# Eight-core hybrid trunk (pooling mixer and gated linear attention): launch, unit changes, gate input, sums of squares and end rearranged

## The reference

```
h = concat(meta, x)
for i in range(4):
    h = h + (pool_mixer, gla_mixer)[i % 2](rmsnorm(h, norm[i]))
out = rmsnorm(h, final_norm)[:, 16:]

pool_mixer: u, z = split(h @ w_in)                       # 2048 channels each
            t = trailing_mean(u, w) - u                  # w = 2, 4, 8, 16 by group of 512 channels
            y = (t @ w_grp[g]) * scale * silu(z);  return y @ w_out
gla_mixer:  q, k, v, z, glr = split(h @ w_in)            # 4 heads, dk 256, dv 512, glr of rank 16
            log_a = log_sigmoid(glr @ w_gate2 + b) / 16
            by chunk: cum = cumsum(log_a); qe = q*exp(cum); ke = k*exp(-cum)
                      o = mask(qe ke^T) v + qe S;  S = exp(g_tot)*S + (k*exp(g_tot-cum))^T v
            o = o * rsqrt(mean(o^2) + eps) * head_norm * silu(z);  return o @ w_out
```

## Time and profile before

| what | us |
|---|---|
| time, median of 3 runs | 2346.13 |
| the three runs | 2346.13, 2355.87, 2049.5 |
| profiled execution, its own time | 2046.73 |
| its span, slowest core (2039.7 to 2045.2 over the cores) | 2045.2 |
| TensorE's mean granted clock, over the cores | 0.994 to 0.997 |
| busy on the slowest core: PE, DVE, ACT, POOL | 1949.3, 1540.1, 1147.1, 258.6 |

### The profile page before, as it was taken

How to read it: one execution, slowest core, us unless ns; L and a number is a source line. 1 busy time by engine, 2 the same in 40 slices (tenths; PEclk the granted TensorE clock), 3 DMA queues, 4 the chain that set the end, 5 groups by cost and what they waited for, 6 DMA issues and landing times.

```text
span 2045.2 us, 55011 instructions; the slowest of 8 cores (2039.7 to 2045.2 us)
## 1 busy us (share of the span) xinstructions
PE 1949.3 (95%) x20056; PEld 1415.8 (69%) x20056; DVE 1540.1 (75%) x2848; ACT 1147.1 (56%) x2482; POOL 258.6 (13%) x411
## 2 busy tenths in 40 slices
PE   5899999999999999999999999999899999999997
PEld 3576677766777767767767767776677676776664
DVE  5768777877777777777777778787777677776887
ACT  3433323467666666667754322344766666666776
POOL 2320000011111111111121100001111111111110
PEclk9999999999999999999999999999999999999999
DMA  9532405050031040040040404131300500400111
GB/s 270 127 46 40 72 2 83 1 84 2 2 61 36 2 80 7 2 74 2 2 74 1 85 1 73 29 55 31 54 2 12 84 2 3 83 2 2 43 64 63
DMA packets 16173, 89.94 MB, mean 44 GB/s; under 512 B 2546, under 2 KB 2802, under 8 KB 7460
## 3 DMA queue, kind: packets, MB, share of 16 engines
q0 software_dynamic: 9136, 59.45, 17.9%
q1 hardware_dynamic: 6772, 26.98, 4.0%
HBM read 137.47 MB, written 8.39 MB: 71 GB/s over the span
## 4 chain that ended last, share of the span: by engine, by line
PE 74%; ACT 10%; DVE 6%; issue 6%; DMA 2%; SPq 1%; POOL 0%; ACTq 0%; DVEq 0%; POOLq 0%
PE ps L461 20%; PE ps L528 11%; PE ps L737 9%; PE ps L751 8%; PE ps L889 8%; PE ps L707 8%; PE ps L313 2%; PE ps L840 2%; DVE arena L851 2%; DMA h<-x 2%; PE ps L808 2%; DVE arena L830 2%; ACT arena L763 1%; ACT arena L762 1%; ACT arena L812 1%
## 5 line engine op out<-in xcount | busy, mean ns | idle before, releaser
L461 PE MATMUL ps<-hnT,W 128*128 128x256 bf16 (+1 forms) x4096 | 463.8, 273 | 3.9 <-ACT arena L473 2.7
L461 PEld LDWEIGHTS ps<-hnT,W 128*128 128x128 bf16 x4096 | 399.6, 98 | 67.0 <-issue 5.0
L726 POOL TENSOR_SCALAR arena<-arena 128x128 bf16<-128x128 bf16 (+1 forms) x272 | 159.4, 586 | 1066.2 <-DVE arena L830 900.1
L889 PE MATMUL ps<-W,arena 128*128 128x512 bf16 (+1 forms) x1056 | 266.3, 380 | 2.7 <-DVE arena L830 2.4
L751 PEld LDWEIGHTS ps<-hnT,W 128*128 128x128 bf16 x4224 | 242.9, 98 | 32.0 <-issue 1.7
L897 DVE SCALAR_TENSOR_TENSOR h<-ps,arena,h 128x512 f32<-128x512 f32 (+1 forms) x264 | 198.0, 750 | 81.6 <-ACT arena L875 54.7
L528 PE MATMUL ps<-W,arena 128*128 128x512 bf16 (+1 forms) x1088 | 248.3, 381 | 11.5 <-POOL W L1034 7.8
L737 PE MATMUL ps<-W,hnT 128*128 128x512 bf16 (+1 forms) x1088 | 258.2, 380 | 0.0
L707 PE MATMUL ps<-hnT,W 128*128 128x128 bf16 (+1 forms) x4288 | 256.8, 217 | 0.0
L751 PE MATMUL ps<-hnT,W 128*128 128x128 bf16 (+1 forms) x4224 | 253.4, 218 | 0.0
L707 PEld LDWEIGHTS ps<-hnT,W 128*128 128x128 bf16 x4288 | 239.8, 98 | 6.3 <-issue 0.6
(11 more groups left out here) (89 smaller groups left out, 2511.7 us busy)
## 6 DMA issues: line engine op xcount, KB each, us to landing
W<-wpack POOLq DMA_DIRECT2D x53, 1024.0 KB, 17.4
h<-x SPq DMA_DIRECT2D x8, 1024.0 KB, 22.4
out<-h SPq DMA_DIRECT2D x16, 512.0 KB, 2.6
h<-wpack SPq DMA_DIRECT2D x4, 1024.0 KB, 23.0
W<-wpack POOLq DMA_DIRECT2D x7, 512.0 KB, 14.0
W<-wpack SPq DMA_DIRECT2D x3, 1024.0 KB, 15.2
gbc<-pool_norm SPq DMA_DIRECT2D x2, 512.0 KB
gbc<-gla_norm SPq DMA_DIRECT2D x2, 512.0 KB
```

Of the source, the lines that this page charges most:

```text
L461: ins = e.matmul(dst[:, f, 0:n], lhsT=Wm[:, 2 * q + f, kc, :], rhs=hnT[:, kc, c0:c0 + n], start=(kc == 0), stop=(kc == 7))
L726: P.op("pool", lambda e, dc=dc: e.tensor_scalar(out=kdT[par][:, dc, 0:n], in0=ke[par][:, dc, 0:n], scalar1=Eq[par][:, dc, n - 1:n], scalar ...
L889: ins = e.matmul(pout[0:n, :], lhsT=yT[par][:, ec, 0:n], rhs=Wo[:, ec, half * 512:(half + 1) * 512], start=(ec == 0), stop=(ec == 3))
```

## The change

- Launch: the SP queue begins with the first two pieces of unit 0, then meta, the norm's gains and x; the fourth piece of x comes ahead of the last two pieces of the unit; `load_unit(1)` moves from before the first block into `late_loads` in block 1. Tile 0 is normalised first, the first two folds come ahead of tile 1, and ACT instead of DVE rounds the second half of Wz.
- Pooling, first block of a layer: the second norm step moves between the u and the z matmuls of the second pair (`mid`). Where a GLA layer's tail is pending, both matmul groups of the first pair come ahead of it.
- `gla_preload` is split; the second part (rounding of the gate's bias on DVE, constant rows of `glrT` on ACT, two loads) comes two blocks later.
- GLA: `gate_in` moves from the head of a step to behind E; F writes bank 0 instead of 4, but for the layer's last chunk; K at a head's first chunk comes behind E; the last chunk of a head has no Q3, K and K2; in the last layer C comes ahead of Zm in the step after chunk 0; `final_tile_b` moves from ahead of Zm to behind C and G1; the last step issues Z's first pass ahead of the state copy, and its F moves to the layer's tail. The tail's first tile of O is followed by the norm step.
- End: the last tile's final product and store go in two halves on two queues.

```diff
@@ stageA
+                zmm = lambda: P.op("pe", lambda e: mm(e, Wz, pzz), rd_h + [Wb[s][1]] + ([b_wz] if ui == 0 else []), PB(2, 3))
+                if before is not None:
                     zmm()
                 P.op("pe", lambda e: mm(e, Wc, pu), rd_h + [Wb[s][0]] + b_Wc[s], PB(0, 1))
+                if before is not None:
+                    before()
...
+                if mid is not None:
+                    mid()
+                if before is None:
                     zmm()
@@ pool run
-                G["A"](bi, 0, k == 0 and before is not None)
-                if k == 0 and before is not None:
-                    before()
+                G["A"](bi, 0, before if k == 0 else None)
...
-                G["A"](bi, 1)
+                G["A"](bi, 1, None, (lambda: slot(False)) if k == 0 else None)
...
-                slot(False)
+                if k > 0:
+                    slot(False)
...
+                if not lastl and k == NBLK + 3:
+                    gla_preload2((li + 1) // 2)
                     load_gvec(gla_norm[(li + 1) // 2:(li + 1) // 2 + 1, :])
@@ stageF
-                P.op("pe", mss, [b_o2, b_one], PB(4))
+                P.op("pe", mss, [b_o2, b_one], PB(pbi))
@@ gla run
+                bare = prev and fuse_final and steps[k - 1][1] == 0
                 if hd == 0:
-                    norm.gate_in(3)
                     stepper = norm
...
                     call("Y", k - 1)
                     call("Su", k - 1)
+                    if more:
+                        call("D2", k - 1)
+                if bare:
+                    call("C", k)
+                call("Zm", k)
+                if not more:
+                    call("Z0", k)
                     call("D2", k - 1)
-                if k >= 2:
-                    maybe_final(k - 2, 1)
-                call("Zm", k)
                 if k == 0 and before is not None:
-                    before()
-                if stepper is not None:
+                    before(lambda: norm.step(3, False))
+                elif stepper is not None:
                     stepper.step(3, False)
-                call("K", k)
-                call("C", k)
+                if ci > 0:
+                    call("K", k)
+                if not bare:
+                    call("C", k)
...
+                if k >= 2:
+                    maybe_final(k - 2, 1)
                 if prev:
                     done_e(k - 1)
+                if ci == 0:
+                    call("K", k)
+                if hd == 0:
+                    norm.gate_in(3)
                 call("K2", k)
-                call("Z", k)
+                call("Z", k, begun=not more)
...
-            call("F", NS - 1)
             call("Dz", NS - 1)
             call("Y", NS - 1)
-        def tail():
+        def tail(mid=None):
+            call("F", NS - 1, pbi=4)
             done_e(NS - 1, roots=False)
@@ launch
+    stage(0, st1[:, 4096:6144], w0[:, 8192:10240], [Wb[1][2]])
+    stage(1, v4(st1[:, 0:4096])[:, :, 0:512], v4(w0[:, 0:4096])[:, :, 0:512], [Wb[1][0]])
+    P.dma("sp", s_meta, [(lambda q: q.dma_start(out=h[0:NMETA, 0, :], in_=meta[:, :]), [], [hb[0]])])
+    load_gvec(pool_norm[0:1, :])
     load_x(0, "sp")
...
     load_x(2, "sp")
+    load_x(3, "sp")
     stage(5, hfl[:, 13 * D:15 * D], w0[:, 12288:14336], [hb[13], hb[14]])
     stage(6, hfl[:, 15 * D:17 * D], w0[:, 14336:16384], [hb[15], hb[16]])
-    load_x(3, "sp")
+    cast("pool", W0[:, 8192:10240], st1[:, 4096:6144], [Wb[1][2]], [Wb[0][2]])
+    cast("dve", v4(W0[:, 0:4096])[:, :, 0:512], v4(st1[:, 0:4096])[:, :, 0:512], [Wb[1][0]], [b_half[0]])
+    n0.prep(0)
+    n0.scale(0)
+    for dc in range(2):
+        fold(0, dc, dc, "act" if dc % 2 else "dve", [b_half[0]])
+    n0.step(6, False)
+    n0.prep(1)
+    for dc in range(2, 4):
+        fold(0, dc, dc, "act" if dc % 2 else "dve", [b_half[0]])
+    n0.scale(1)
+    cast("act", v4(W0[:, 0:4096])[:, :, 512:1024], v4(st1[:, 0:4096])[:, :, 512:1024], [Wb[1][1]], [b_half[1]])
+    n0.step(7, False)
+    n0.scale(2)
+    for dc in range(4, 8):
+        fold(0, dc, dc, "act" if dc % 2 else "dve", [b_half[1]])
+    n0.step(7, False)
     cast("dve", W0[:, 4096:6144], hfl[:, 9 * D:11 * D], [hb[9], hb[10]], [Wb[0][1]])
-    cast("dve", W0[:, 6144:8192], hfl[:, 11 * D:13 * D], [hb[11], hb[12]], [Wb[0][1]])
+    cast("act", W0[:, 6144:8192], hfl[:, 11 * D:13 * D], [hb[11], hb[12]], [b_wz])
...
     def late_loads():
...
         load_x(6, "sp")
         load_x(7, "sp")
+        load_unit(1)
     n0.prep(3)
     n0.scale(3)
-    if len(units) > 1:
-        load_unit(1)
```

More of the change, by code:

```diff
@@ L534, in stageO @@
                             in1=po[0:nt, :], op=ALU.add), PB(pbi) + [hb[ti]], [hb[ti]])
+                    if mid is not None and ti == tiles[0]:
+                        mid()
                 if g == 3 and not lastl and bi < 6:
@@ L1100, in build @@
     pending()
-    P.wait_all("sp", hb[1:])
+    P.wait_all("sp", hb[1:] + b_half)
     P.emit(nc, E)
```

86 lines of the change are left out of this document (45 added, 41 removed).

## The result

The changed kernel takes 2022.01 us (median of 20 runs, lowest 2020.04), the kernel before 2059.59 on the same chip (median of 20, lowest 2047.53). The ratio is 0.985, 95% interval 0.982 to 0.988. The profiled execution took 2020.69 us, its slowest core (core 5) 2019.1; so 26.0 us are won against the 2046.73 that the sum was made against, where 38.2 were forecast.

The account below looks back on a forecast made before the run. PE, busy 1949.3 of 2045.2 us, was taken as the bound, with about 87 us of named waits. Terms summing to 38.2 off 2046.73 gave 2008.5, predicted as 2009; own range 2003 to 2017, wider range 1997 to 2030.

Parts of the forecast that it names:

- rival 3: Launch keeps its pace, through folds at 1.2 GHz or DVE's order: gains 3 instead of 8.5 us, 2014; chance 0.16.
- rival 2: Only launch and last head count (18 us); small gains go into the next wait: 2028 us; chance 0.14.
- Part 4: First heads: moving the gate input ends G's wait, a closed ACT and DVE loop sets steps of 10.25; 5 us.
- Part 5: Last head: new order and bank end F's wait for the mask product, step 9.46 to 8.7; 9.7 us.
- Part 1: Launch: earlier x piece and new order let block 0's O start at about 51.7 instead of 59.53; 8.5 us.
- Part 2: GLA to pool: free matmuls ahead of the last chunk's F win 2.6, the moved norm step 1.3; 3.9 us.
- part 3: Preload: the gate bias's rounding two blocks later ends O's wait behind DVE; 3.7 us.
- Part 6: Small ones: head begins, C ahead of Zm, tail order and the end; 2.5, 1.9, 1 and 2 us.
- Part 7: F in bank 0: costed at nothing, with some 0.8 us of cover left before the next Q overwrites the bank.
- Rival 1: The first heads' loop has a way out and PE sets their pace: another 10 to 17 us, 1996; chance 0.13.

Follow-up runs that it names:

- run 1: Changed kernel with the whole old launch section (loads, roundings, order of folds and norm steps) put back; mean core span 2012.7 us, 2.0 less than the changed kernel.
- run 2: Changed kernel with layer 2's pscale read early, during layer 1's head 1, into its own buffer; mean core span 2011.7 us, 3.0 less than the changed kernel.
- run 3: Changed kernel with the gate's input product back at the head of the first heads' steps; mean core span 2022.8 us, 8.1 more than the changed kernel.
- run 7: Changed kernel with F's sums back in bank 4 and the final product's second half back ahead of Z; core spans 2026.1 us, ratio 0.992 to the kernel before.
- run 8: Changed kernel with 20 idle products behind the fourth fold and 4 behind the next norm step; mean core span 2014.3 us, against the changed kernel's 2014.7.
- run 9: Changed kernel with tile 2's norm step between the sixth and seventh fold, in bank 2; mean core span 2013.7 us, 1.0 less than the changed kernel.
- run 11: Changed kernel with the late roundings issued ahead of the squares and roots of tiles 7 and 8; mean core span 2011.5 us, 3.2 less than the changed kernel.
- run 12: Changed kernel with the edits of run 2, run 4, run 8, run 9 and run 11, and POOL rounding Wz's second half; 2006.82 us, 0.979 of the kernel before.
- run 4: Changed kernel with the gate's input product one place further, behind G2 instead of ahead of Z; mean core span 2006.4 us, 8.3 less than the changed kernel.
- run 5: Changed kernel with only F's sums of squares back in bank 4; mean core span 2014.0 us, against the changed kernel's 2014.7.
- run 6: Changed kernel with only the second half of the last head's final product back ahead of Z; mean core span 2015.1 us, against the changed kernel's 2014.7.

## Why the prediction was right, and where it was not

2022 lies in the range of 1997 to 2030 and 13 us above the forecast of 2009. It lies outside the forecast's own range (2003 to 2017, given 0.53) and fits no rival by itself: the launch's 3 of rival 3 would give 2014, and rival 2 (2028) counts on the launch and gives the small parts nothing, where they gave most. That the total is no further off is in part luck: parts 4 and 5 gave 5 us more than forecast, against 16 less elsewhere. The terms, by the stages above and the runs:

| part | forecast | measured | by |
|---|---|---|---|
| 1 launch | 8.5 | 0.2 at O(0), 1.6 over many cores; none in the whole kernel | stages, run 1 |
| 2 GLA to pool | 3.9 | 3.0 | stages |
| 3 preload | 3.7 | 2.0 in layer 0; 2.0 in layer 2, together with part 2's norm step | stages, run 2 |
| 4 gate input | 5 | 8.1 (9.7 by the stages of run 3) | stages, run 3 |
| 5 last head | 9.7 | 11.6 | run 7 |
| 6 small ones | 7.4 | 4.1, a remainder | the rest of the stages |
| 7 F in bank 0 | 0 | 0 | no wait of Q for ACT |
| layer 2's new wait | none | -3.7 | run 2 |
| sum | 38.2 | 27.3 | the stages' medians give 27.1 |

**Part 1 is the step that failed** (8.5 us forecast, 0.2 to 1.6 measured at O(0)). The forecast let PE reach the stall 3 us sooner and took what stood before block 0 as unchanged. It had followed data and DVE, and not two things in PE's own order: tile 2's norm step now comes behind the eighth fold, in that fold's bank, where nothing hides its transposes and ACT's copy (2.0 us, runs 8 and 9), and the idle time between the groups of folds costs clock (1.6 us in the median, up to 2.9, run 8). So block 0 starts 1.1 us later instead of 3 sooner. Behind it, the norm step that was moved to save 1.3 us waits 2.20 itself (L388 for tile 4 at 44.21, core 5). The other half of the 8.5 was to be POOL's rounding at 49.5. It started at 52.6 to 59.3 over the cores, because the roots of tiles 7 and 8 stand ahead of it on POOL and wait for DVE (3.46 us on core 5); run 11 took some 6 us of this away by order alone. The data was late by less: the fourth piece of x landed at 38.6 to 43.6 for the 37 forecast, the last weight piece at 45.4 to 49.5 for 45. And the clock had nothing to give at the first O: its 24 matmuls take 6.94 us at a granted clock of 1.00 in run 11 (median of the cores), 7.10 at 0.69 in the kernel before, so the 2 us that the forecast counted as lost were 0.2. The 51.7 forecast for O(0) was within reach: it is the median of run 12, with four edits of the launch that the change doesn't have. This is rival 3, at 7 to 8 us where it was given 5.5: the slow folds and an engine's order that holds block 1 are the reasons that it named, and tile 2's norm step behind the last fold, 2.0 us, is one that it did not.

The rule weighed there, in "TensorE: Matmul & The Clock Gate" of the Trainium skill (the array falls back to half clock when it idles), was right in kind: the 16 products took 3.61 us at 1.00 on core 3, where PE had stood 1.81 and 0.22 us in the two waits ahead of them, and 5.95 at 0.60 on core 5, where it had stood 3.59 and 2.10; run 8 filled these gaps and had 3.61 or 3.62 on all eight cores. That is 2.3 of the 3.4 us that the prediction worked out, and not on all cores.

**Layer 2** was in no part and no rival. The prediction wrote that with GLA to pool the 32 free matmuls come first; it didn't ask what POOL's queue does at that point. The tail of the GLA layer, which ends with unit 9's loads, now stands ahead of the pooling block's running sum on POOL. Unit 9's loads, which before stood behind POOL's running sum and went out at 1043.61, are issued from 1023.41 on (core 5; core 3 for the kernel before), and the small load of SP's queue has them for company. The loads of a moved piece have to be followed like its other instructions.

**Part 4** is right by its mechanism and a little better than its number: 10.14 a step for 10.25, the steps with a sum of squares from 11.13 to 10.14; 0.11 less in each of 28 steps is the 3.1 us by which 8.1 exceeds 5. Rival 1 (PE sets the pace) was not true of the change and was made true by run 4, for 7 us rather than 10 to 17, as PE's own step is 9.9.

**Part 5**: 8.58 a step for 8.7. What the forecast could not say, and runs 5 to 7 do, is that bank and order each do the whole of it.

**Part 2 and part 3** gave 7.0 of 7.6. The 3.0 are in the stage that ends with layer 1, where F's wait was, forecast at 2.6. Of the 1.3 for the moved norm step nothing is seen: L461's wait for L473 is gone, and the step waits 1.2 for DVE in its place, in run 2 too. The 2 us in layer 2 (375.0 to 373.0 in run 2) are covered in the changed kernel by the wait for pscale; how they divide between the two parts was not tried.

**Part 6** lost 3.3 us. At the heads' begins of layer 3 the wait did move to Y, as forecast, and 1.7 are left each time of the 1.6 to 1.9 that K waited and the 0.2 of Y; in layer 1 it moved from K (0.3 to 0.6) to E's wait for the mask (0.5 to 0.8), and the heads 1 and 2 there are 0.7 us longer in sum. D's wait for the mask (3.1) is gone, as forecast, and L407's for L391 stayed (1.2 of 1.3), as it was not. The end gave 0.4 for 2: E's wait for Y is 2.15 for 1.89, and the clock gave back 0.1 of the 1 us hoped for.

**Part 7**: no wait of Q (L716) for ACT in the list of after, and the old bank (run 5) changes nothing by itself.

## What to carry to other kernels

When a step is moved, list what stands behind it on every queue at its new place, and above all the loads: bulk loads that come sooner in their engine's order go out sooner, and a small load that something waits for within some 10 us has to be issued well before them (it took up to 12.5 us here). In a launch, the wait that is removed shows the next one in program order; follow each engine's order to the first block before a gain is counted, and put the step that needs one engine's round trip between two matmul groups, not behind the last. Two edits against one wait are not two gains: here either alone is worth all of it.

## What the runs showed of the chip

An 8 KB load takes 1.5 to 1.8 us from issue to landing on all eight cores when nothing else is in flight (kernel before), 3.1 to 5.2 in a quiet stretch of layer 1, right behind a load on its own queue (run 2), and 6.9 to 12.5 with two or three loads of 1 MB and one of 512 KB from another queue in flight (the changed kernel). The trace of core 5 shows that it is the load's own packets that come late. There are 144 of them, none in the first 4.4 us behind the issue (in the kernel before all are done within 1.4, on every core), and then they run among the bulk packets until 12.06 us, 0.45 before the landing. Queues of core 5 from 1038.8 to 1046.5 (packets, MB, share of 16 engines):

```profile
q0 software_dynamic: 174, 1.29, 99.6%
q1 hardware_dynamic: 144, 0.01, 2.6%
```

The Trainium skill, "DMA: Bandwidth & Descriptors", "Queues, rings and completion order", says that a DMA engine takes its queues in turn, packet by packet, and the trace agrees in so far as it has both queues' packets side by side in this stretch. That does not make the load cheap: 144 packets are nine for each of 16 engines if they are spread evenly, and with one bulk packet of 0.6 us (median of this core, up to 1.6) ahead of each that is 5.6 us, an estimate; from the first packet to the end of the last it took 7.6. On three cores (0, 3, 4) the last of the small packets is done after 6.4 to 7.4 us, on the other five after 11.2 to 12.2; layer 2 takes 373.0 us on the three and 376.4 to 377.6 on the five. Why the first packet is 3.6 to 4.9 us late, and what parts the three cores from the five, stays open.

DVE pauses at a few places for no reason that the profile names. In the changed kernel the two state updates of one step of layer 3 stand 0.46 us apart, where they follow at 0.10 as a rule. It is the same step on all eight cores, and in nine of the twelve other runs too; in runs 1, 9 and 12 there is no such pause on this line, and the kernel before has it once as well, on all its cores, at a step of layer 1. Timeline of core 3; the step is 10.50 instead of 10.14.

```profile
1483.03 0.74 DVE L873 SCALAR_TENSOR_TENSOR arena<-arena,ps 128x512 f32<-128x512 f32 x1
1484.23 0.75 DVE L873 SCALAR_TENSOR_TENSOR arena<-arena,ps 128x512 f32<-128x512 f32 x1 [0.46 <-DVE arena L873]
```

Between kernels whose heads are the same the heads differ by 0.3 to 1.2 us each, the same on all cores of a kernel, and some of their steps by 0.14 to 0.36. Pauses of this kind could explain it, among others the 2.4 us by which run 1's heads are shorter; that is not shown. What they are, and whether the code ahead of them moves them, was not tried and stays open.
